# Rows of the normalised operand 1280 bytes apart instead of 1088, behind a lead of 64 bytes

## What is computed

```python
def swiglu(h, wg, wu, wd):
    return (jax.nn.silu(h @ wg) * (h @ wu)) @ wd
h = modulate(rms_norm(x, ln_ffn1[i]), sh1, sc1)
x = x + 0.5 * g1[:, None, :] * swiglu(h, ffn1_wg[i], ffn1_wu[i], ffn1_wd[i])
```

## Time and profile before

| what | value |
|---|---|
| median of 3 runs | 1509.7 us (1507.81 to 1510.53) |
| profiled execution, whole time | 1507.29 us |
| its span | 1505.5 us |
| PE busy | 1473.1 us, 98% of the span |
| DVE busy | 1177.2 us, 78% |
| ACT busy | 820.0 us, 54% |
| mean granted clock of PE | 0.998 |

### The profile page before, as it was taken

How to read it: one execution, slowest core, us unless ns; L and a number is a source line. 1 busy time by engine, 2 the same in 40 slices (tenths; PEclk the granted TensorE clock), 3 DMA queues, 4 the chain that set the end, 5 groups by cost and what they waited for, 6 DMA issues and landing times.

```text
span 1505.5 us, 22326 instructions
## 1 busy us (share of the span) xinstructions
PE 1473.1 (98%) x9258; PEld 1314.9 (87%) x9258; DVE 1177.2 (78%) x1394; ACT 820.0 (54%) x998; POOL 49.6 (3%) x40
## 2 busy tenths in 40 slices
PE   7999999899999999999999899999999999999998
PEld 6888889898888998888888888889888889988887
DVE  6988889689889778889767798898866566786654
ACT  6655354575553575554577665555655445565442
POOL 1000015200000000000000000000000000000000
PEclk9999999999999999999999999999999999999999
DMA  8988955279889559889534398897655555465551
GB/s 287 310 295 287 339 194 167 84 250 313 297 284 330 178 191 303 296 289 311 168 113 142 128 304 294 288 325 253 191 188 182 184 166 169 141 221 180 186 184 68
DMA packets 275972, 341.69 MB, mean 227 GB/s; under 512 B 6931, under 2 KB 256939, under 8 KB 275872
## 3 DMA queue, kind: packets, MB, share of 16 engines
q1 hardware_dynamic: 273904, 334.74, 67.3%
q0 software_dynamic: 1968, 5.54, 1.1%
HBM read 339.18 MB, written 2.63 MB: 227 GB/s over the span
## 4 chain that ended last, share of the span: by engine, by line
PE 86%; DVE 7%; ACT 4%; issue 1%; DMA 1%; DVEq 0%; SPq 0%; ACTq 0%
PE banks L1691 43%; PE banks L1692 22%; PE banks L1623 5%; PE banks L1624 5%; PE banks L1625 5%; DVE w_lo L993 1%; ACT w_hi L536 1%; DVE xn L1064 1%; DVE ada_acc L1111 1%; ACT xs L566 1%; DVE x_res L1137 1%; PE banks L1763 1%; ACT xn L555 1%; DVE xs L1012 1%; DMA ada<-in_ada_w 0%
## 5 line engine op out<-in xcount | busy, mean ns | idle before, releaser
L1691 PE MATMUL banks<-xs,w_hi 128*128 128x512 f32 x1952 | 682.7, 393 | 3.2 <-DVE w_lo L993 3.0
L993 DVE TENSOR_TENSOR w_lo<-raw,w_hi 128x2048 fp32r<-128x2048 f32 (+1 forms) x241 | 537.9, 2237 | 161.5 <-ACT w_hi L536 161.3
L536 ACT ACTIVATE w_hi<-raw 128x2048 fp32r<-128x2048 f32 (+1 forms) x249 | 464.8, 1870 | 214.9 <-PE banks L1692 169.7
L1692 PE MATMUL banks<-xs,w_lo 128*128 128x256 f32 x1952 | 547.6, 281 | 0.0
L1691 PEld LDWEIGHTS banks<-xs,w_hi 128*128 128x128 f32 x1952 | 366.4, 188 | 88.4 <-DVE w_lo L993 4.3
L1691 PE MATMUL banks<-g_pair,w_hi 128*128 128x512 f32 x1056 | 366.9, 391 | 0.0
L1692 PEld LDWEIGHTS banks<-xs,w_lo 128*128 128x128 f32 x1952 | 366.8, 188 | 0.0
L1692 PE MATMUL banks<-g_pair,w_lo 128*128 128x256 f32 x1056 | 295.7, 280 | 0.0
L1691 PEld LDWEIGHTS banks<-g_pair,w_hi 128*128 128x128 f32 x1056 | 197.5, 187 | 43.2
L1692 PEld LDWEIGHTS banks<-g_pair,w_lo 128*128 128x128 f32 x1056 | 199.6, 189 | 0.0
L1111 DVE SCALAR_TENSOR_TENSOR ada_acc<-ada,c_act,ada_acc 128x1152 f32<-128x1152 f32 x124 | 175.2, 1413 | 12.3 <-DMA ada<-in_ada_w 9.7
(11 more groups left out here) (302 smaller groups left out, 1694.9 us busy)
## 6 DMA issues: line engine op xcount, KB each, us to landing
ada<-in_ada_w SPq DMA_DIRECT2D x128, 576.0 KB, 6.9
raw<-in_ffn_wg SPq DMA_DIRECT2D x44, 1024.0 KB, 5.5
raw<-in_ffn_wu SPq DMA_DIRECT2D x44, 1024.0 KB, 5.5
raw<-in_ffn_w_in SPq DMA_DIRECT2D x43, 1024.0 KB, 7.1
raw<-in_ffn_wd SPq DMA_DIRECT2D x32, 1024.0 KB, 5.2
raw<-in_ffn_w_out SPq DMA_DIRECT2D x16, 1024.0 KB, 6.4
raw<-in_ffn_wd SPq DMA_DIRECT2D x16, 768.0 KB, 4.9
raw<-in_attn_w_qkv SPq DMA_DIRECT2D x12, 1024.0 KB, 5.3
```

The source lines that it names most:

```text
L536: act.activation(w_hi[:, s, 0:width(c)], raw[:, s, 0:width(c)], ACT.Copy).then_inc(hi_ready, 1)
L993: dve.tensor_tensor(w_lo[:, s, 0:width(c)], raw[:, s, 0:width(c)], w_hi[:, s, 0:width(c)].bitcast(F32), ALU.subtract).then_inc(lo_ready, 1)
L1691: pe.matmul(o, wh[:, k, m], pair, start=first, stop=False, skip_group_check=True)
L1692: return pe.matmul(o[:, 0:T], wl[:, k, m], pair[:, 0, :], start=False, stop=last, skip_group_check=True)
```

## The change

Rows of `xs` are now T + 64 = 320 elements (1280 bytes) apart, and ahead of the first row lies a lead of 16 elements (64 bytes). `xs` grows by 3136 bytes. Room comes from three places: the part of `ada` beyond 14 x 256 elements goes, since `b_mix`, which lay in it, now lies in the arena; three of the six constants (`tri`, `low_mask`, `up_mask`) go from `consts_sb` into the arena of the mixing stage. The constants are loaded by two DMAs in place of one, and the waits ask for both. The FILL matmuls read the three constants that are left, 384 columns instead of 512.

```diff
-XS_ROW = T + 16
+XS_ROW = T + 64
+XS_LEAD = 16
...
-        xs = sb("xs", [P, 2, KT, XS_ROW], F32R)
+        xs_flat = sb("xs", [P, XS_LEAD + 2 * KT * XS_ROW], F32R)
+        xs = xs_flat[:, XS_LEAD:XS_LEAD + 2 * KT * XS_ROW].rearrange("p (a k t) -> p a k t", a=2, k=KT)
         xs_hi, xs_lo = xs[:, 0, :, 0:T], xs[:, 1, :, 0:T]
...
-        ada_flat = sb("ada", [P, 4 * D])
+        ada_flat = sb("ada", [P, 14 * T])
...
-        consts = sb("consts_sb", [P, 6, P])
-        tri, low_mask, up_mask, ident, causal, pair_ones = (consts[:, i, :] for i in range(6))
+        consts = sb("consts_sb", [P, 3, P])
+        ident, causal, pair_ones = (consts[:, i, :] for i in range(3))
...
         w_glr = carve(KT * 16).rearrange("p (k n) -> p k n", k=KT)
+        masks = carve(3 * P).rearrange("p (i n) -> p i n", i=3)
+        tri, low_mask, up_mask = (masks[:, i, :] for i in range(3))
...
-        b_mix = ada_flat[0:2, 2 * D + KT * P:2 * D + 2 * KT * P]
+        top[0] = KEPT
+        b_mix = carve(KT * P, 2)
...
-            pool.dma_start(consts[:, :, :], a["consts"]).then_inc(consts_in, 16)
+            pool.dma_start(consts[:, :, :], a["consts"][:, 3:6, :]).then_inc(consts_in, 16)
+            pool.dma_start(masks, a["consts"][:, 0:3, :]).then_inc(consts_in, 16)
...
-                dve.wait_ge(consts_in, 16)
+                dve.wait_ge(consts_in, 32)
...
                     for _ in range(FILL):
-                        pe.matmul(bank[MISC][:, :], ones_d[:, :], consts[:, 0:4, :], start=True, stop=True,
+                        pe.matmul(bank[MISC][:, 0:3 * P], ones_d[:, :], consts[:, :, :], start=True, stop=True,
                                   skip_group_check=True)
```

More of the change, by code:

```diff
@@ L1732, in norm @@
                 if n and not after:
-                    pe.wait_ge(consts_in, 16)
+                    pe.wait_ge(consts_in, 32)
                 if JOINT[n]:
```

## The result

The changed kernel takes 1518.46 us (median of 4 runs, 1518.21 to 1518.66), the kernel before on the same chip 1509.41 us (1507.81 to 1510.53): ratio 1.0061, 95% interval 1.0046 to 1.0076, so 0.6% slower. The profiled execution has a span of 1516.8 us against 1505.5.

A forecast was written before the change was run, and what follows sets the result against it. PE, busy 98% of the span, was taken to bound the kernel. 8.2 + 1.8 + 1.0 - 0.5 = 10.5 us less than 1507.3 gave 1496.8; with 2.4 for the median, 1499. Range for 8 in 10: 1487 to 1523.

The forecast's parts named there:

- at 345.0: Joined pairs on `xs` and `g_pair`: with rows at phase 192, 345.0 ns a pair, from 349.2 and 346.7.
- The bounds beside it: Shortest and longest pair taken for phase 192, 342.5 and 355.5 ns: on `xs`, 13.1 us less to 12.3 more.
- the order that 117 of the 122 chunks have: Reason for taking 345.0: its two source pairs stand in the order of most chunks, 1872 of 1952 pairs.
- -8.2 and -1.8: Forecast changes in us from phase 192: 1952 pairs on `xs` 8.2 less, 1056 pairs on `g_pair` 1.8 less.
- `g_pair` shows that an even phase holds one pitch: Step within the bad-phase rival: rows all at one phase keep a single pitch, as `g_pair` at 346.7 ns.
- the even phase is the bad one: Rival, chance 0.31: phase 192 behind phase 192 makes pairs on `xs` and `g_pair` slower, 1516 to 1531 us.
- mild form: Bad-phase rival with pairs at 350.75 ns, the mean of four pairs: 7.3 us more less 1 for triples, 1516.
- full form: Bad-phase rival with pairs at 355.5 ns on `xs` and `g_pair`: 21.6 us more, 1531.
- near 397: Sign of a wrong prediction: pair matmul durations even but near 397 ns; the forecast mean on `xs` was near 389.
- No effect: Rival, chance 0.14: pairs end between 347.6 and 349.6 ns, the time within 3 us of 1509.7.
- The triples: 192 triples on `cs` go from 361.4 to 356.0 ns, 1.0 us less; the 352 on `xs` keep their pitch.
- The supply: Case of a faster PE held up by DVE and DMA: 0.5 us off the gain; losing half gives 1504.5.

The follow-up runs named there:

- the fast version: Against the changed kernel, the 64-byte lead goes from ahead of `xs` to ahead of `w_lo`; 1488.77 us, ratio 0.9883 to the kernel before.

## Why the prediction was wrong

**The step that failed** is "at 345.0", the pitch of an even phase of 192. I had made it out of two single pairs, 342.5 and 347.5, that stood in a sequence of mixed phases. The bounds beside it, 342.5 and 355.5, held: the measured means, 352.5 on `xs` and 352.7 on `g_pair`, lie between them. But the value between them was chosen by resemblance ("the order that 117 of the 122 chunks have"), and that was no reason.

It was not the small sample that failed. By their starts the two pairs are 344 and 346 ns (single durations give a pitch only to 1.5 ns), and in the whole third network of the kernel before the pairs of k = 1 and k = 5, phase 192, have means of 345.8 and 344.2. The step from a mixed sequence to an even one failed. The same trace could have warned of it: there the eight k have, from each pair's start to the next, 348, 346, 348, 354, 357, 344, 350 and 345 ns in turn, so two rows of phase 128 (k = 0 and 4) are 9 ns apart and two of phase 64 (k = 3 and 7) also. A short pair in a mixed sequence can owe its length to its neighbours. The earlier trace rows pointed the other way: 355.5 behind a pair of the same phase is close to the middle one of 357, 355, 348; that may be chance.

**The sum with these**: 1952 x (352.5 - 349.2) = 6.4, 1056 x (352.7 - 346.7) = 6.3, triples -2.6 (below): 10.1 us more, where the two spans differ by 11.3 us and the medians by 9.1. I had -8.2 and -1.8.

**The second step that failed** is "`g_pair` shows that an even phase holds one pitch". It did in that kernel; with all rows at that very phase the same tile had 346.7 in one network and 353.4 in another.

**The rival "the even phase is the bad one"** (0.31) is what happened. Its mild form, a mean of 350.75, gave 1516, its full form 1531; 352.6 lies between, and so does 1518.5. Its mechanism was half right: the pitch depends on what ran before, but not as "behind a pair of its own phase"; there are several lasting patterns. Of the signs of being wrong, the mean duration came out "near 397" (396), but the durations were not even (392 to 398 in one stretch); the conclusion that I had tied to that, that the phase modulo 256 is not what counts, was wrong too.

**"No effect"** (0.14) is out. The prediction names two rules of the Trainium skill beside it, from "SBUF — State Buffer", section "SBUF: two separate sides", and "TensorE: Matmul & The Clock Gate", section "Step-by-step: what each phase is for". What it drew from them, that the place of a row is indifferent, does not hold here: 64 bytes moved from ahead of `xs` to ahead of `w_lo` are worth 30 us. Whether the rules themselves fail, no run shows.

**The triples** went as forecast on `cs`: 48 of them take 17.07 us (1299.56 to 1316.63), 355.6 ns, 5.8 less than in the earlier trace rows against the 5 expected. The 80 on `xs` went from 356.0 to 354.5 (211.76 to 240.12). 192 x 5.8 + 352 x 1.5 = 1.6 us. The 160 with `xs` as weights, which I had left at their pitch, went from 354.0 to 347.5 ns where they follow each other without a wait: 1.0 us.

**Constants, FILL, overlays at 0**: right, by their rows and by the run with the rows undone, which is within 0.1% of the kernel before.

**The supply**: 0.5 us was taken off for a faster PE; PE became slower and the case did not come up. In the fast version PE's idle time ahead of the `xs` pairs, nearly all of it a wait for low weights, is 4.6 us in all against 3.2, with a span 20 us shorter; the limit was farther away than I feared.

## What to carry to other kernels

When PE is busy all the time, look at the starts of consecutive matmuls, not only at their mean duration: if they are not all alike, the place in memory of the moving rows and of both weight tiles is worth trying, at one run with a profile per setting. Move one tile at a time by 64 bytes, and measure a long even stretch; do not carry a pitch from a mixed sequence over to an even one. An edit that only makes rows "even" says nothing of where they lie against the weights, and the latter is what paid here.

## What the runs showed of the hardware

- Matmul pairs of the same shape, at the 2.4 GHz level, took 340.0, 346.7, 348.9, 350.0, 351.1, 352.0 or 353.3 ns in long even stretches, by the places modulo 256 bytes of low weights and moving row, with the high weights at 128 (or all moved together). That it is modulo 256 and not more is shown by the changed kernel itself: `xs` rows 1280 apart and `g_pair` rows 1024 apart have one pattern. Triples took 340 to 360 ns.
- Moving all of them together by 64 bytes changed neither the triples' pitch (359.7 ns) nor the set of patterns (346.7 and 353.3).
- The pitch was the same, 353.3 ns, with DVE busy 8.9 us of 10 and the DMA engines 0.81 of their time as with DVE busy 2.5 us of 10 and no DMA.
- At some places two patterns exist, up to 10 ns a pair apart (340.0 and 350.0). A stretch keeps its pattern over more than a hundred microseconds, and nine small matmuls or one pair with its two matmuls swapped can change it.
- Why the places act (what in the chip two of these reads meet in) no run here shows; it stays open, and so does which pattern a stretch falls into.
